# Third down projection with tokens on the partitions, last norm per token tile, residual turned inside that feed-forward

## What is computed

```python
def rms_norm(x, g):
    xf = x.astype(jnp.float32)
    y = xf * lax.rsqrt(jnp.mean(xf * xf, axis=-1, keepdims=True) + EPS)
    return (y * g.astype(jnp.float32)).astype(x.dtype)
...
        h = rms_norm(x, norm_ffn_pre[l])
        f = (jax.nn.silu(h @ w_gate[l]) * (h @ w_up[l])) @ w_down[l]
        x = x + rms_norm(f, norm_ffn_post[l])
    return x
```

## Time and profile before

| | |
|---|---|
| profiled execution | 2127.72 us |
| its span (first to last instruction) | 2125.9 us |
| granted TensorE clock, mean | 0.978 of full |
| PE busy | 1991.0 us (94%), 8941 matmuls |
| PEld (weight loads, beside PE) | 1613.4 us (76%) |
| DVE (VectorE) | 977.3 us (46%) |
| ACT (ScalarE) | 512.3 us (24%) |
| POOL (GpSimd) | 1450.9 us (68%) |
| DMA queues' mean | 77 GB/s, 25.4% of 16 engines' span |
| instruction DMA | 0.69 MB and 0.23 MB, 0.1% and 0.0% |
| chain that ended last | PE 76%, DVE 12%, POOL 6%, issue 3%, ACT 2%, DMA 1% |

### The profile page before, as it was taken

One profiled execution on the slowest core, in us unless ns is written; L12 is line 12 of the kernel. 1 busy time (PEld: TensorE's weight loads), 2 busy tenths in 40 slices (PEclk: granted clock), 3 DMA queues, 4 the chain that ended last, 5 costly groups with the idle time before them and its releaser, 6 DMA issues.

```text
span 2125.9 us, 26050 instructions
## 1 busy us (share of the span) xinstructions
PE 1991.0 (94%) x8941; PEld 1613.4 (76%) x8941; DVE 977.3 (46%) x1198; ACT 512.3 (24%) x920; POOL 1450.9 (68%) x1662
## 2 busy tenths in 40 slices
PE   7999999999999989889999999999898879999996
PEld 6788888777777877777788888876677648888884
DVE  6432330687655477656432331057766573333004
ACT  3111100343444422430211110023555331111001
POOL 5777777776665656447777777776555568777771
PEclk9999999999999999999999999999999979999998
DMA  5333322332211223003333332242100113333320
GB/s 173 89 97 91 98 99 89 84 86 72 60 50 51 69 70 90 11 24 96 89 97 92 98 99 99 94 104 50 30 21 21 40 40 99 99 92 95 99 89 40
DMA packets 255460, 163.87 MB, mean 77 GB/s; under 512 B 30124, under 2 KB 245230, under 8 KB 255262
## 3 DMA queue, kind: packets, MB, share of 16 engines
q1 hardware_dynamic: 253728, 157.90, 25.4%
q10 hardware_dynamic: 1662, 5.06, 0.6%
HBM read 160.81 MB, written 2.13 MB: 77 GB/s over the span
## 4 chain that ended last, share of the span: by engine, by line
PE 76%; DVE 12%; POOL 6%; issue 3%; ACT 2%; DMA 1%; ACTq 0%; POOLq 0%; DVEq 0%; SPq 0%
PE bank L797 12%; PE bank L798 12%; PE bank L799 12%; PE bank L885 5%; PE bank L886 5%; PE bank L887 5%; PE bank L1056 4%; PE bank L1057 4%; PE bank L1058 4%; POOL w_lo L654 3%; PE bank L952 2%; DVE work L2309 1%; DVE work L2239 1%; POOL w_hi L650 1%; PE bank L1317 1%
## 5 line engine op out<-in xcount | busy, mean ns | idle before, releaser
L654 POOL TENSOR_TENSOR w_lo<-raw,w_hi 128x256 fp32r<-128x256 f32 x1192 | 953.9, 831 | 24.8
L650 POOL TENSOR_SCALAR w_hi<-raw 128x1024 fp32r<-128x1024 f32 x298 | 322.9, 1084 | 420.0 <-PE bank L799 165.1
L797 PE MATMUL bank<-u_hi,w_hi 128*128 128x512 f32 x1056 | 417.1, 395 | 16.9 <-DVE u_lo L2165 15.7
L798 PE MATMUL bank<-u_lo,w_hi 128*128 128x512 f32 x1056 | 413.8, 392 | 0.0
L799 PE MATMUL bank<-u_hi,w_lo 128*128 128x512 f32 x1056 | 413.6, 392 | 0.0
L797 PEld LDWEIGHTS bank<-u_hi,w_hi 128*128 128x128 f32 x1056 | 199.7, 189 | 66.4 <-issue 18.4
L799 PEld LDWEIGHTS bank<-u_hi,w_lo 128*128 128x128 f32 x1056 | 199.9, 189 | 42.2
L798 PEld LDWEIGHTS bank<-u_lo,w_hi 128*128 128x128 f32 x1056 | 200.1, 189 | 41.1 <-issue 0.7
L1056 PE MATMUL bank<-u_hi,w_hi 128*128 128x512 f32 x464 | 193.8, 418 | 2.3 <-DVE u_lo L2165 1.6
L885 PE MATMUL bank<-hid_hi,w_hi 128*128 (+1 forms) x480 | 187.0, 389 | 1.0 <-POOL w_lo L654 1.0
L887 PE MATMUL bank<-hid_hi,w_lo 128*128 (+1 forms) x480 | 186.8, 389 | 0.0
(11 more groups left out here) (513 smaller groups left out, 3263.4 us busy)
## 6 DMA issues: line engine op xcount, KB each, us to landing
raw<-in_w_in SPq DMA_DIRECT2D x52, 512.0 KB, 3.7
raw<-in_ffn_w_gate SPq DMA_DIRECT2D x44, 512.0 KB, 3.7
raw<-in_ffn_w_up SPq DMA_DIRECT2D x44, 512.0 KB, 3.8
raw<-in_ffn_w_down SPq DMA_DIRECT2D x44, 512.0 KB, 3.5
raw<-in_w_gate SPq DMA_DIRECT2D x22, 512.0 KB, 3.7
raw<-in_w_up SPq DMA_DIRECT2D x22, 512.0 KB, 3.7
raw<-in_w_down SPq DMA_DIRECT2D x22, 512.0 KB, 3.7
raw<-in_w_branch SPq DMA_DIRECT2D x12, 512.0 KB, 3.4
```

Of the source, the lines that this page charges most:

```text
L650: pool.tensor_scalar(w_hi[:, s, :], raw[:, k, :], 1.0, 1.0, ALU.mult, ALU.mult).then_inc(hi_done, 1)
L654: pool.tensor_tensor(w_lo[:, s, c], raw[:, k, c], w_hi[:, s, c].bitcast(F32), ALU.subtract).then_inc(low_quarter if quarter < 3 else split ...
L797: pe.matmul(outs[:, 0:n], wh, rhs_hi[:, c, :], start=(c == 0), stop=False)
L798: pe.matmul(outs[:, 0:n], wh, rhs_lo[:, c, :], start=False, stop=False)
```

## The change

In the third feed-forward (`fi == 2`), and behind it:

- Down projection: the stationary operand becomes a 128x128 block of `hid_hi` or `hid_lo` (128 tokens), the moving one 512 columns of the weights. Bank b = 2i + half holds token tile i, output features of one half, with tokens on the partitions. Units 2 to 19 are written out in place of the loop. In the last two units the order of the banks is 0 to 5 for the first, then 0 to 5 for the second, then 6 and 7 for both.
- Residual: `residual_turned` transposes `hT` chunk by chunk, 16 transposes behind two(0) and 16 behind two(1), into banks 4 to 7; `residual_kept` on ScalarE copies them back in place (`h_tok` is at the address of `hT`).
- ScalarE loads the gain of the last norm as a row for all partitions (`gain_row`, 512 KB, in place of `u_hi`) and the square root's table behind its last hidden chunk.
- Norm: ScalarE squares each bank and has the sum over the 512 columns accumulated into `f_sums`. VectorE adds the two halves, ScalarE takes the root, VectorE the reciprocal, all on 128x1, for each token tile. VectorE scales a bank by factor and gain row into `out_tok` (8 instructions of 128x512).
- The residual is added by GpSimd for banks 0 to 5 and by VectorE for 6 and 7. SP stores eight times 256 KB, from a buffer for each tile.
- Gone: the copies to `fT`, the 8 matmuls with ones, root and reciprocal of 128x512, the 8 adds to `hT` on VectorE, the 32 transposes at the end and the 8 copies behind them.

```diff
@@ placements @@
+        h_at = top[0]
         hT = place("hT", [P, KC, S])
+        h_tok = at("h_tok", [P, KC, S], h_at)
...
-        fT = at("fT", [P, KC, S], u_at)
+        gain_row = at("gain_row", [P, D], u_at)
+        f_square = at("f_square", [P, 2 * TT, S], u_at + 4096)
...
-        out_tok = at("out_tok", [P, 2, D], a_at)
+        out_tok = at("out_tok", [P, TT, D], a_at)
...
+        POOL_ENDS = 6
+        def half_of(b):
+            return slice(b % 2 * S, (b % 2 + 1) * S)
+        def kept(b):
+            return h_tok[:, b % 2 * TT:(b % 2 + 1) * TT, b // 2 * P:(b // 2 + 1) * P]
+        def ended(b):
+            return out_tok[:, b // 2, half_of(b)].rearrange("p (c n) -> p c n", c=TT)
@@ SP @@
-            for i in range(TT):
-                sp.wait_ge(o_ready_a, i + 1)
-                sp.wait_ge(o_ready_b, i + 1)
-                sp.dma_start(out[0, i * P:(i + 1) * P, :], out_tok[:, i % 2, :]).then_inc(stored[i % 2], 16)
+            for b in range(2 * TT):
+                if b < POOL_ENDS:
+                    sp.wait_ge(out_pool, b + 1)
+                else:
+                    sp.wait_ge(out_dve, b - POOL_ENDS + 1)
+                i, c = b // 2, half_of(b)
+                sp.dma_start(out[0, i * P:(i + 1) * P, c], out_tok[:, i, c]).then_inc(stored, 16)
@@ GpSimd @@
             run(U_GU3 + SPL, N_UNITS)
+            for b in range(POOL_ENDS):
+                pool.wait_ge(t_gain, b + 1)
+                pool.tensor_tensor(ended(b), ended(b), kept(b), ALU.add).then_inc(out_pool, 1)
@@ TensorE @@
+            def residual_turned(part):
+                for k in range(4):
+                    c = 4 * part + k
+                    if part:
+                        pe.wait_ge(h_kept, k + 1)
+                    elif k == 0:
+                        pe.wait_ge(n_std, N_FPRE + 1)
+                    for i in range(TT):
+                        last = pe.transpose(bank[4 + k][:, i * P:(i + 1) * P], hT[:, c, i * P:(i + 1) * P], ident)
+                    last.then_inc(h_turned, 1)
...
+                if fi == 2:
+                    residual_turned(0)
+                    two(1, False)
+                    residual_turned(1)
+                    start = 2
...
+                def product(m, j, slot, start, stop):
+                    if fi == 2:
+                        t, c = slice(m // 2 * P, (m // 2 + 1) * P), half_of(m)
+                        th, tl = hid_hi[:, j, t], hid_lo[:, j, t]
+                        pe.matmul(bank[m][:], th, w_hi[:, slot, c], start=start, stop=False)
+                        pe.matmul(bank[m][:], tl, w_hi[:, slot, c], start=False, stop=False)
+                        return pe.matmul(bank[m][:], th, w_lo[:, slot, c], start=False, stop=stop)
...
-                with pe.Fori(1, FT // 2 - 1) as it:
-                    for k in range(2):
-                        down(2 * it + k, k, False, False)
+                if fi == 2:
+                    for j in range(2, FT - 2):
+                        down(j, j % 2, False, False)
+                else:
+                    with pe.Fori(1, FT // 2 - 1) as it:
+                        for k in range(2):
+                            down(2 * it + k, k, False, False)
...
+                if fi == 2:
+                    order = [(m, k) for k in range(2) for m in range(6)] + [(m, k) for m in (6, 7) for k in range(2)]
+                else:
+                    order = [(m, 0) for m in range(4, KC)] + [(m, k) for m in range(4) for k in range(2)]
+                    order += [(m, 1) for m in range(4, KC)]
...
             ffn(2, U_GU3, N_FPRE)
-            norm_sum(N_FPOST)
-            pe.wait_ge(n_std, N_FPOST + 1)
-            pe.wait_ge(x_ready, 3 * KC)
-            for i in range(TT):
-                ...
-                        last = pe.transpose(bank[2 * (i % 2) + half][:, c * P:(c + 1) * P],
-                                            hT[:, 4 * half + c, i * P:(i + 1) * P], ident)
@@ ScalarE @@
+            def residual_kept(part):
+                for k in range(4):
+                    c = 4 * part + k
+                    act.wait_ge(h_turned, c + 1)
+                    copy(h_tok[:, c, :], bank[4 + k][:], h_kept)
...
+                if fi == 2:
+                    residual_kept(0)
+                    two(1, False)
+                    residual_kept(1)
                     start = 2
...
             ffn(2)
-            squares(N_FPOST, fT, f_here(2))
-            norm_std(N_FPOST)
-            for i in range(TT):
-                ...
-                copy(out_tok[:, i % 2, 512:1024], bank[2 * (i % 2) + 1][:], o_ready_b)
+            act.wait_ge(unit_done, U_DN3)
+            act.dma_start(gain_row[:], t["norm_ffn_post_2"].to_broadcast([P, D])).then_inc(ld_row, 16)
+            load_root()
+            def token_square(b):
+                if b < 2 * TT - 1:
+                    act.wait_ge(f_tile, 2 * (KC - 1) + b + 1)
+                else:
+                    act.wait_ge(unit_done, N_UNITS)
+                act.activation(f_square[:, b, :], bank[b][:], ACT.Square, accum_out=f_sums[:, b:b + 1]).then_inc(t_sq, 1)
+            def token_std(i):
+                act.wait_ge(t_add, i + 1)
+                act.activation(f_root[:, i:i + 1], f_total[:, i:i + 1], ACT.Sqrt, scale=1.0 / D, bias=EPS).then_inc(t_std, 1)
+            for b in range(2 * TT):
+                token_square(b)
+                if b >= 2 and b % 2 == 0:
+                    token_std(b // 2 - 1)
+            token_std(TT - 1)
@@ VectorE @@
-            ffn(2, U_GU3, N_FPRE, N_FPRE, to_fT)
-            norm_add(N_FPOST, N_FPOST, fT, G_FPOST2, 2 * KC)
-            for i in range(TT):
-                ...
-                dve.tensor_copy(out_tok[:, i % 2, 0:512], bank[2 * (i % 2)][:]).then_inc(o_ready_a, 1)
+            ffn(2, U_GU3, N_FPRE, N_FPRE, None)
+            dve.wait_ge(ld_row, 16)
+            def token_rows(i):
+                dve.wait_ge(t_sq, 2 * i + 2)
+                dve.tensor_tensor(f_total[:, i:i + 1], f_sums[:, 2 * i:2 * i + 1], f_sums[:, 2 * i + 1:2 * i + 2],
+                                  ALU.add).then_inc(t_add, 1)
+                dve.wait_ge(t_std, i + 1)
+                dve.reciprocal(f_root[:, i:i + 1], f_root[:, i:i + 1]).then_inc(t_rec, 1)
+                dve.wait_ge(t_rec, i + 1)
+                for b in (2 * i, 2 * i + 1):
+                    dve.scalar_tensor_tensor(out=out_tok[:, i, half_of(b)], in0=bank[b][:], scalar=f_root[:, i:i + 1],
+                                             in1=gain_row[:, half_of(b)], op0=ALU.mult, op1=ALU.mult).then_inc(t_gain, 1)
+            for i in range(TT):
+                token_rows(i)
+            for b in range(POOL_ENDS, 2 * TT):
+                dve.wait_ge(t_gain, b + 1)
+                dve.tensor_tensor(ended(b), ended(b), kept(b), ALU.add).then_inc(out_dve, 1)
```

More of the change, by code:

```diff
@@ L129, in two_blocks @@
         best8 = place("best8", [P, TT, 8])
+        f_sums, f_total, f_root = (place(n, [P, 8]) for n in ("f_sums", "f_total", "f_root"))
         root_one = place("root_one", [P, 8])
@@ L290, in two_blocks @@
                              "ld_c"))
-        stored = [sem("stored0"), sem("stored1")]
+        stored, ld_row = sem("stored"), sem("ld_row")
+        t_sq, t_add, t_std, t_rec, t_gain = (sem("t_" + n) for n in ("sq", "add", "std", "rec", "gain"))
+        h_turned, h_kept = sem("h_turned"), sem("h_kept")
         gain_zero, gain_t, gain_ready, const_r, xt_done, x_ready, trig, trig_a = (
@@ L813, in _ @@
             U = (u_hi, u_lo)
[L815 to L819, removed]
             def sum_total(ni, b):
@@ L824, in sum_total @@
                 pe.matmul(bank[b][:], ones, total_of(ni), start=True, stop=True).then_inc(n_acc, 1)
[L826 to L829, removed]
             def norm_wait(ni):
@@ L875, in ffn @@
                 d0 = u0 + 2 * FT
+                def product(m, j, slot, start, stop):
[5 more added lines that the diff above has]
+                        return pe.matmul(bank[m][:], th, w_lo[:, slot, c], start=False, stop=stop)
+                    wh = w_hi[:, slot, m * P:(m + 1) * P]
+                    wl = w_lo[:, slot, m * P:(m + 1) * P]
+                    pe.matmul(bank[m][:], wh, hid_hi[:, j, :], start=start, stop=False)
+                    pe.matmul(bank[m][:], wh, hid_lo[:, j, :], start=False, stop=False)
+                    return pe.matmul(bank[m][:], wl, hid_hi[:, j, :], start=False, stop=stop)
                 def down(j, slot, start, stop):
@@ L882, in down @@
                             pe.wait_ge(f_up, fi * FT + FT)
[L883 to L887, removed]
+                        last = product(m, j, slot, start, stop)
                     last.then_inc(unit_done, 1)
@@ L902, in ffn @@
                         pe.wait_ge(f_lo, fi * FT + FT)
[L903 to L909, removed]
+                    last = product(m, FT - 2 + k, k, False, k == 1)
+                    if x == last_first or (m, k) == (KC - 1, 1):
```

(16 more changed lines are left out.)

31 lines of the change are left out of this document (8 added, 23 removed).

## The result

The changed kernel takes 2140.06 us (median of 5 runs, 2137.94 to 2142.26) against 2128.71 us (2127.31 to 2130.94): ratio 1.0052, 95% interval 1.0037 to 1.0067. It is slower; I had forecast 2107.7 us. Its profiled execution took 2137.94 us with a span of 2136.0 us, 10.1 us longer than before.

What follows compares the result with a forecast made beforehand. TensorE, busy 94% of the span, bounds the kernel, with a serial tail of 33.7 us behind its last matmul. Tail -24.8 and transposes +3.8 give -21.0 us: 2107.7 us, range 2104 to 2113.

Steps and rivals of the forecast that it cites:

- Part two: Down projection: swapped operands, 18 written-out units and the gain row's load cost nothing; 528 matmuls stay at 0.227 us.
- Rival C: Written-out units: matmuls over 0.049 us slower, through fetching or unhidden weight loads, would cancel the gain; chance 0.03.
- Part one: Residual's two sets of 16 transposes, moved amid feed-forward matmuls: a loss of 3.8 us; ScalarE's eight copies cause no wait.
- Part three: Order of the last two down-projection units: six banks instead of five done before the last low weights, 0.68 us less.
- Part four: New tail around the last matmuls: VectorE sets the pace at 2.19 us a tile; end at 2101.1 us.
- Rival A: Tail: GpSimd's adds hold up VectorE's scalings at the shared port, adding 5 to 6 us, 2113 us; chance 0.06.
- B: Third feed-forward: the transposes let TensorE's clock fall, two sets costing 6 us, 2114 us; chance 0.05.
- D: Tail: sums per tile don't run under the last matmuls, scaling starts 5 us later, 2112.7 us; chance 0.05.
- The sum: Whole kernel: -24.8 us of tail and +3.8 for transposes give -21.0 us, span 2104.9, time 2107.7 us.

Runs made afterwards that it cites:

- its moved copy: The kernel before with only the three small tiles placed ahead of `work`, unused, so activations lie 128 bytes higher: 2161.88 us against 2128.27, ratio 1.016.
- the kernel not moved: The changed kernel with its three small tiles placed behind all others, so activations lie where they lay before: 2107.16 us against 2128.27, ratio 0.9907; again 2107.47 us.

## Why the prediction was wrong, step by step

- *Part two, the down projection and "nothing, then".* This is the step that failed, by what it leaves out. I priced every instruction of the diff and none of its placements. Three `place` calls moved the activations from 0 to 128 modulo 256 bytes against the weights, and TensorE's distance grew from 0.2267 to 0.2324 or 0.2333 us in all three feed-forwards, and by as much where the projections multiply 512 columns. The term that I put at nothing is 33.6 us by itself in the kernel before and 32.9 in the changed one: -21 + 33 is the result.
- *"I cost the swap of operands at zero", and the code written out at zero.* Right: with the old placement the changed down part holds 222 matmuls in 50 us as in the loop, where the earlier trace rows has 223.
- *Rival C* had the right sign and the wrong place. It put the slower distance into the 18 written-out units and asked for 0.049 us more there. There were 0.0066 us more in 528 down matmuls (3.5 us), and 0.0057 in thousands of others. I had closed it with the earlier trace rows, which was sound for fetching but says nothing of where an operand lies: at its 256 columns the distance is 0.118 us in the kernel before and in its moved copy alike. My chance for slower, 0.03, was a chance for a mechanism in the touched stretch only; a cause that works on the whole kernel had none.
- *Part one*: 3.3 us by the trace, 3.1 to 4.3 by leaving them out, where I had 3.8. Right in kind, by the trace a little too dear. The copies on ScalarE hid as said.
- *Part three*: held. The wait for the last split shrank and six banks were ahead of it: in the kernel not moved the first matmul that needs the last unit's low weights starts at 2088.69, 0.51 us behind the one before it, an ordinary distance and 0.28 us of wait; in the kernel before the same distance was 1.18 us, so 0.67 us are gone where I had 0.68.
- *Part four*: 15.3 us from the first square to the end, where I had 15.7 (2101.1 - 2085.4). Errors cancel in it, which is luck: 0.39 us more for each of three tiles, because the sum waited for GpSimd; against that 2.4 us in place of 3.0 to the first scaling (squares at 0.70 us in place of 0.80 among it), 1.2 in place of 1.8 for VectorE's two last adds, and 2.5 in place of 3.0 from its last instruction to the end. The scalings were free of the lock and took 0.747 us each, 1.41 for two.
- *Rival A*: not the scalings; but the rule of the Trainium skill that I quoted beside it, page "SBUF — State Buffer", section "SBUF: two separate sides", names the instructions that did block, those with two SBUF inputs beside a GpSimd instruction that reads SBUF, and makes no exception for small ones. The trace agrees, with 0.78 us and more for a sum that takes 0.16 alone. I had applied it to the two last adds alone and not to the sums.
- *Rivals B and D*: no sign of either. The clock stays 1.00 behind the transposes, and in the kernel not moved the first tile is scaled from 2092.08 us, while TensorE works on until 2095.6.
- *The sum*: it gives 2107.7 us, and with the placement as before 2107.2 and 2107.5 were measured. It was a right sum for another program, and that it is so close is in part the luck of part four.

## What to carry to other kernels

A line that allocates is part of a change, even if the tile is 32 bytes and hardly used: write down where every operand of TensorE lies before and after, and put new small tiles behind the large ones. When a change costs time before the point it touches, don't look at waits first; count instructions in a stretch where the engine is 100% busy in both traces. And an experiment that does only the placement costs one line and settles it.

## What the runs showed of the hardware

- The distance of two 128x128 by 512 fp32r matmuls, at full clock with hidden weight loads, follows the SBUF address of the moving operand minus that of the stationary one, modulo 256 bytes: 0.2267 to 0.228 us at 0, 0.2267 at -16 (240), 0.229 at 64, 0.231 to 0.235 at the other multiples of 16. The absolute address doesn't matter (everything moved by 128 bytes: ratio 1.0001). Why it does so no run here shows, nor whether other types behave alike. At 256 columns the kernel's matmuls stood 0.118 us apart before and in the copy moved by 128 bytes, so there it doesn't show. In this kernel 2.5% on the pace are 1.6% on the time.
- The same difference gave 0.2324 us in some feed-forwards and 0.2333 in others of the same trace (the moved kernel before: 432 in 100 us from 1850 us, 430 from 1100 us). What chooses between them stays open.
- A VectorE instruction of one column with two SBUF inputs took 0.16 us alone and 0.78 to 1.15 us beside GpSimd's adds; with one tensor input and a scalar operand 0.20 or 0.21 us in both cases.
- The accumulated sum of a ScalarE instruction is an instruction of its own in the trace, 0.19 us, of which some 0.10 us came on top of each square (squares start 0.70 us apart).
